# VectorE's key products spread over four steps, block preparation moved two steps later, two value taps joined

## The reference, cut to what matters

```python
qkv = silu(centred_depthwise_conv(qkv, conv_w))        # five taps
q, k, v = split(qkv)                                   # q, k normalised per head
gc = cumsum(g)                                         # log decays, per direction
decay = exp(where(incl, gc[:, None] - gc[None, :], -inf))
kb = k * beta[..., None]
a_low = where(strict, einsum("id,jd->ij", kb, k) * decay, 0.0)
lower = a_low + eye(c)
sol = triangular_solve(lower, rhs, unit_diagonal=True)  # rhs from v and k
attn = einsum("id,jd->ij", q, k) * decay
```

## Time and profile before

| | |
|---|---|
| median of 3 runs | 2287.91 us |
| the profiled execution, its own time | 2289.45 us |
| its span, first to last instruction | 2287.1 us |
| granted TensorE clock, mean | 0.998 |
| busy: TensorE / VectorE / ScalarE / GpSimd | 99% / 63% / 55% / 16% |
| VectorE in slices 2 to 11 of 40 (57 to 629 us), busy tenths | 6 to 8 |

### The profile page before, as it was taken

How to read it: one execution, slowest core, us unless ns; L and a number is a source line. 1 busy time by engine, 2 the same in 40 slices (tenths; PEclk the granted TensorE clock), 3 DMA queues, 4 the chain that set the end, 5 groups by cost and what they waited for, 6 DMA issues and landing times.

```text
span 2287.1 us, 33236 instructions
## 1 busy us (share of the span) xinstructions
PE 2267.3 (99%) x10565; PEld 1889.2 (83%) x10565; DVE 1446.8 (63%) x2465; ACT 1267.9 (55%) x2303; POOL 360.5 (16%) x698
## 2 busy tenths in 40 slices
PE   9999999999999999999999999999999999999997
PEld 7888888888888888888888888888888888888886
DVE  6678788787766555555655655566555555566554
ACT  6566475574456544455554555546565444556544
POOL 0010100000332410013421100021233000242100
PEclk9999999999999999999999999999999999999999
DMA  9655365464577766677766675667777666777665
GB/s 335 182 157 161 114 168 139 137 186 117 172 209 213 219 204 194 195 203 220 218 209 206 203 218 157 167 206 222 211 220 216 198 193 195 212 220 211 204 194 158
DMA packets 253035, 443.84 MB, mean 194 GB/s; under 512 B 38124, under 2 KB 40045, under 8 KB 252781
## 3 DMA queue, kind: packets, MB, share of 16 engines
q1 hardware_dynamic: 231709, 420.15, 62.7%
q0 software_dynamic: 20480, 21.01, 2.8%
q10 hardware_dynamic: 720, 1.06, 0.1%
HBM read 419.00 MB, written 2.10 MB: 184 GB/s over the span
## 4 chain that ended last, share of the span: by engine, by line
PE 93%; DVE 3%; ACT 1%; DMA 1%; issue 1%; POOL 1%; SPq 0%; POOLq 0%; ACTq 0%; DVEq 0%
PE pair L566 29%; PE pair L568 29%; PE pair L567 29%; PE aux L766 3%; PE aux L577 2%; DVE w_lo L1601 1%; DVE r L1946 1%; PE aux L813 0%; DMA raw<-in_dn_w_in 0%; POOL xn_late L2427 0%; DVE attnT L1940 0%; DVE projections L1846 0%; ACT r L1323 0%; PE aux L697 0%; PE aux L714 0%
## 5 line engine op out<-in xcount | busy, mean ns | idle before, releaser
L1601 DVE TENSOR_TENSOR w_lo<-raw,w_hi 128x512 fp32r<-128x512 f32 x1536 | 1025.2, 692 | 640.4 <-ACT w_hi L1064 636.9
L1064 ACT ACTIVATE w_hi<-raw 128x512 fp32r<-128x512 f32 x1536 | 945.7, 633 | 803.4 <-DMA raw<-in_ffn_w 630.4
L566 PE MATMUL pair<-w_hi,xT 128*128 128x512 f32 x1984 | 781.6, 394 | 4.2 <-DVE w_lo L1601 1.9
L568 PE MATMUL pair<-w_hi,xT 128*128 128x512 f32 x1984 | 772.9, 390 | 0.0
L567 PE MATMUL pair<-w_lo,xT 128*128 128x512 f32 x1984 | 772.4, 389 | 0.0
L566 PEld LDWEIGHTS pair<-w_hi,xT 128*128 128x128 f32 x1984 | 372.6, 188 | 84.2 <-issue 3.4
L568 PEld LDWEIGHTS pair<-w_hi,xT 128*128 128x128 f32 x1984 | 372.4, 188 | 78.4
L567 PEld LDWEIGHTS pair<-w_lo,xT 128*128 128x128 f32 x1984 | 372.8, 188 | 74.6
L566 PE MATMUL pair<-w_hi,hid_hi 128*128 128x512 f32 x1012 | 393.8, 389 | 0.1
L568 PE MATMUL pair<-w_hi,hid_lo 128*128 128x512 f32 x1012 | 393.7, 389 | 0.0
L567 PE MATMUL pair<-w_lo,hid_hi 128*128 128x512 f32 x1012 | 393.7, 389 | 0.0
(11 more groups left out here) (255 smaller groups left out, 1164.6 us busy)
## 6 DMA issues: line engine op xcount, KB each, us to landing
raw<-in_ffn_w SPq DMA_DIRECT2D x1024, 256.0 KB, 3.2
raw<-in_dn_w_in SPq DMA_DIRECT2D x208, 256.0 KB, 2.9
raw<-in_tok_w_out SPq DMA_DIRECT2D x128, 256.0 KB, 3.2
raw<-in_gm_w_in SPq DMA_DIRECT2D x112, 256.0 KB, 2.9
xn_late<-xn_late POOLq DMA_DIRECT2D x640, 32.0 KB, 3.0
raw<-in_mem_w_kv SPq DMA_DIRECT2D x64, 256.0 KB, 3.3
r<-in_mem_columns SPq DMA_DIRECT2D x8, 256.0 KB, 5.4
h<-in_x_columns SPq DMA_DIRECT2D x8, 256.0 KB, 5.6
```

Of the source, the lines that this page charges most:

```text
L566: pe.matmul(acc, act_hi[:, kt, tokens], w_hi[:, slot], start=start, stop=False)
L568: mm = pe.matmul(acc, act_lo[:, kt, tokens], w_hi[:, slot], start=False, stop=last and k == 1)
L1064: act.activation(w_hi[:, slot], raw[:, slot], ACT.Copy).then_inc(hi_ready, 1)
L1601: dve.tensor_tensor(w_lo[:, slot], raw[:, slot], w_hi[:, slot].bitcast(F32), ALU.subtract).then_inc(tiles_split, 1)
```

## The change

Three engines' steps are renumbered; no instruction is added or removed. Step numbers below are VectorE's unless said otherwise.

- The `yield` in the loop over key products moves one level in: one bank for each of steps 3 to 6, where there were two in each of steps 3 and 4.
- The second value tap goes from step 5 to step 7.
- Block preparation (L1959 to L1968) goes from step 6 to step 8, where `attention_part` and `mix_pairs(2, 3)` of the third group follow it in the same step.
- The third value tap goes from step 7 to step 9, in front of the fourth.
- On ScalarE, the block rows (L1337) go from step 6 to step 7 and the copy back (L1351) from step 7 to step 8, in front of `attention_part` and `mix_pairs(2, 3)`.
- TensorE's steps, and every engine's steps from 10 on, stay as they were.

```diff
@@ -1329,6 +1329,7 @@
                 yield
                 yield
                 yield
+                yield
                 for m in range(2):
                     drained(act, at(DG + 2 * m))
                     drained(act, at(DG + 2 * m + 1))
@@ -1351,7 +1352,6 @@
                     free(act.activation(NT[:, 1, m].rearrange("p h i -> p (h i)"), bank(n)[:], ACT.Copy), n)
                 for m in range(2):
                     drained(act, at(DH + m))
-                yield
                 attention_part()
                 mix_pairs(2, 3)
                 yield
@@ -1967,9 +1967,6 @@
                 dve.wait_ge(sem("block_parts"), g * 2 + 1)
                 dve.tensor_tensor(blk_lo, blk.rearrange("p x c -> p (x c)"), blk_hi.bitcast(F32), ALU.subtract
                                   ).then_inc(sem("block_parts"), 1)
-                yield
-                values_taps(2)
-                yield
                 attention_part()
                 mix_pairs(2, 3)
                 yield
@@ -1993,6 +1990,7 @@
                             dve.tensor_tensor(blk[:, :, 0:row], blk[:, :, 0:row], blk_term[:, :, 0:row], ALU.add
                                               ).then_inc(made, 1)
 
+                values_taps(2)
                 values_taps(3)
                 yield
                 eliminate(0, 1)
```

## The result

The changed kernel takes **2298.91 us** (median of 4 runs, 2298.1 to 2299.8) where the kernel before takes 2288.41 us in the same comparison: ratio 1.0046, 95% interval 1.0033 to 1.0058. That is 10.5 us slower; 2292.2 us with a range up to 2296.5 was forecast. The profiled execution took 2298.1 us, its span is 2295.2 us.

A forecast was written before the change was run, and what follows sets the result against it. TensorE, busy in 99% of the span, was taken as the bound. Group costs of 0.3, 1.6 and 2.4 us, with 2.10 us won inside them, gave +4.3 on the median 2287.91: 2292.2 us, range 2288.0 to 2296.5.

The forecast's parts named there:

- main mechanism: ScalarE's block rows move behind its gates drain, so block_parts comes 11.0 us behind slab 7's start, TensorE after 9.1.
- ScalarE's table load: Ahead of the gates drain: 1.28 us, forecast to begin near 337.6 and end before slab 7 finishes, so free.
- Waits at slab 7: TensorE between slabs 6 and 7: waits of 1.56, 0.25 and 0.29 us vanish, -2.10 us in three groups.
- From the drain's start to `block_parts`: Chain of drain, block rows, w_hi and split of slab 10, preparation and last signal: 8.0 us together.
- The drain starts 3.0 us behind the start of slab 7: ScalarE's gates drain waits for slab 7's 12 products, the last one's record and the signal: 3.0 us.
- third rival: The table switch is not free: 1.28 us more in each chain, at most +3.8 us, 2296 us; chance 0.04.
- The three groups: Net cost by group, first, second and third: +0.3, +1.6 and +2.4 us, summing to +4.3 us.
- Third group, eliminations: Two taps in step 9 free slot 2's bank later, so TensorE waits 1.25 us at slot 6.
- The 2.66 us for a table switch: Skill rule weighed for ScalarE's drain: it would start 0.5 to 1.1 us later per group; judged contradicted by the trace.
- First rival: TensorE never waits for block_parts and the 2.10 us are won: 2285.8 us; chance 0.08.
- Second rival: VectorE's later steps 8 to 11 delay slot 6 or slabs 13 to 16 in all groups: 2297 us; chance 0.10.
- Fourth rival: The change does nothing, as VectorE is held by TensorE's banks: 2287.9 us; chance 0.03.

The follow-up runs named there:

- e4: The changed kernel, but VectorE takes the key products two banks in each of steps 3 and 4 again, steps 5 and 6 empty; 2302.92 us, ratio 1.0063.
- e1: The changed kernel, but in ScalarE's gates drain the wait for slab 7 is written ahead of the wait for the norm; 2293.99 us, ratio 1.0023.
- e3: The changed kernel with five products of zeros on TensorE in each group just ahead of its wait for block_parts; 2296.76 us, ratio 1.0036.
- e2: The changed kernel, but ScalarE takes the gates drain three slabs later, behind the split of slab 12; 2288.7 us, ratio 1.0002.
- e6: The kernel before with only the third value tap moved from step 7 to step 9, in front of the fourth; 2290.02 us, ratio 1.0006.
- e8: e1 with the fourth value tap moved from step 9 to VectorE's empty step 12; 2293.38 us, ratio 1.0022.
- e10: e1 with three products of zeros on TensorE in each group ahead of its wait for block_parts; 2292.51 us, ratio 1.0019.

## Why the prediction was wrong

The direction of the forecast's centre and its main mechanism held; the time lies 2.4 us above the range. The step that failed is ScalarE's table load, which the sum counted as free; it measured 1.3 to 1.6 us in each group. A second cost, the clock, is not in the sum at all. The steps one by one:

- **Waits at slab 7, -2.10 us.** Right: the distance from slab 6 to slab 7 is 2.72 us in all three groups, and e4 brings the waits back.
- **From the drain's start to `block_parts`, 8.0 us.** Right: 343.01 to 351.15, 8.14 us.
- **The drain starts 3.0 us behind the start of slab 7.** Wrong, and the step that failed: 4.26 us (338.75 to 343.01). The prediction took the table load as free, since "after the change it begins near 337.6" while ScalarE waits. It began at 341.72, behind the wait for slab 7. The row that it argued from, the load at 340.17 right behind the rounding, could not tell the two apart: slab 7 was over by then. The third rival named exactly this and its price, 3.8 us at most, with a chance of 0.04. With e1 the term is measured: 1.33 us in the second group, where the clock was 2.4 GHz in both (6.72 us from the start of slab 9 to that of slab 10, and 8.05 in the changed kernel).
- **The clock.** Missing from the sum, and from the rivals. In the first group the 16 products of step 9 took 2.82 us (194.94 to 197.76), where the second group's took 1.99 (351.15 to 353.14), and slab 10 took 0.67 us more: 1.5 us. In the trace of before a wait of 1.56 us had not lowered the clock, and no wait of some 3 us stood in these groups. The Trainium skill, "TensorE: Matmul & The Clock Gate", section "What's actually happening", says that the throttled clock is the default and activity releases it. The traces agree, as e3 keeps the clock up by products of zeros alone. The same page of the Trainium skill warns, in its section "HAM oscillation — how this bites in real kernels", of gaps in TensorE's work that let the clock fall. That would have been a rival against this change.
- **The three groups.** Right once the load and the clock are out of the way: e1 has +0.43, +1.70 and +2.55 us, where 0.3, 1.6 and 2.4 were forecast. This is more than luck, since the terms fit as well.
- **Third group, eliminations.** Right where it could show: 1.25 us forecast for the wait at slot 6, 1.26 us in e1. In the changed kernel the longer wait in step 9 and the slow clock took its place, so it added nothing.
- **The 2.66 us for a table switch** of the Trainium skill, "ScalarE: Activation LUTs", section "What ACT_TABLE_LOAD costs". Not borne out: the SiLU starts 0.01 us behind the end of the load (341.72 + 1.28, 343.01), and the load's 1.28 us are all that the chain pays in the second group (1.33 by e1).
- **First rival (the chain fits):** wrong. It needed 6.1 us from the start of the drain, and 8.14 were measured. With the drain out of the way, in e2, there is still nothing won. **Second rival (VectorE's backlog):** true for the third group, 1.0 us (e6). In the first the margin of 0.2 us that the prediction had was missed by 0.16 us (4.31 us from slab 12 to slab 13 in e1, 4.15 before). **Fourth rival (nothing happens):** ruled out by the interval, 1.0033 to 1.0058.

The account of the change, by the groups, takes the versions as steps from before to the change. First, +4.7 us net from the block rows' place behind the drain and the second tap of step 9, the waits at slab 7 won (e1). Then +4.2 us from the three table loads (e3 less e1: 1.30, 1.29 and 1.63). Last, +1.4 us from the clock in the first group (the change less e3). These are 10.3 by construction; what supports them is that two of the three loads come to within 0.02 us of the 1.28 us recorded. In the third group the load started 0.36 us behind the end of slab 7's last record (498.52 to 498.88), in the second 0.09; that is most of the 0.35 us more there, and why it did so stays open. In the third group the clock and slot 6 stand for each other: e3's third group is as long as the change's.

What stays open: which waits let the clock fall. The second group's 3.35 us did not in the profiled execution, 1.86 us in e8 did.

## What to carry to other kernels

When a step is moved in an in-order queue, look at what it now stands behind, and take that neighbour's own waits, its table load included, as part of the chain. A table load ahead of an activation can be held by a wait that the program wrote for the activation, as here. Write the late wait first (in e1 this freed the load in all three groups), or find a trace in which the partner was late, before counting the load as hidden. Where TensorE sets the time, give each new wait of two or three microseconds a chance of the slower clock behind it too: here 1.4 us in one group and nothing in the two others.

## What the runs showed of the hardware

- The clock's cost is not added to every other cost: a slow stretch ahead of a wait is paid by that wait. In the third group it cost nothing (+4.15 us with it, +4.18 in e3 without).
- Products of zeros on TensorE kept the granted clock at 2.4 GHz in the three groups of both profiled executions that had them (e3, e10), and the spread of the times was smaller with them: 4.4 us in e1, 2.7 us in e10.
- The clock did not always fall behind the same wait: 1.86 us lowered it in e8 and not in e1.
- A table load of 1.28 us started only once the wait written last ahead of its activation was over (341.72 in the changed kernel), and ran ahead of the one written first (337.94 in e1).
- In the third group each reordering of VectorE's taps only moved a wait: 1.26 us at slot 6 (e1) or 1.3 us at slab 16 (e8).
